# Retention: the product of masked scores and values in high and low parts, one modulation step and one reciprocal moved

## The reference, cut to what matters

```
s   = einsum(q, k) * decay            # masked scores, per head
o   = einsum(s, v)                    # the product that is changed
var = mean(square(o - mean(o)))       # group norm over the 512 channels
ro  = (o - mu) * rsqrt(var + eps);  ro = ro * gn_g + gn_b
ret_out = (silu(rg) * ro) @ w_ret_out
mod = silu(c) @ w_ada + b_ada         # "modulation", a matrix-vector product
```

## Time and profile before

| | us |
|---|---|
| runs before, median of 3 | 2944.29 |
| profiled execution | 2945.46 |
| its span | 2943.7 |
| PE busy | 2844.9 (97%) |
| DVE busy | 1749.9 (59%) |
| ACT busy | 989.7 (34%) |

### The profile page before, as it was taken

The page is one execution under the profiler, slowest core; times in us unless marked ns, Lnnn a source line. Parts: engine busy times, 40 slices in busy tenths (PEclk is TensorE's granted clock), DMA queues, the critical chain, the costliest instruction groups (busy, mean ns, idle before and its releaser), DMA issues.

```text
span 2943.7 us, 37223 instructions
## 1 busy us (share of the span) xinstructions
PE 2844.9 (97%) x15519; PEld 2444.4 (83%) x15519; DVE 1749.9 (59%) x2406; ACT 989.7 (34%) x1371; POOL 121.2 (4%) x157
## 2 busy tenths in 40 slices
PE   6999999999899999999989999999999988999999
PEld 5888887979788888789878888888888977888887
DVE  6655755554566777566487565665555348454454
ACT  4333333232333222332276232222213337332222
POOL 0100000000001100000000000000000000000000
PEclk9999999999999999999989999999999999999999
DMA  7343444545234644343510212233322251223232
GB/s 247 125 135 106 130 146 143 174 117 159 88 116 119 198 149 130 100 130 114 135 38 15 86 53 92 92 100 96 100 65 83 68 115 37 65 79 93 93 108 72
DMA packets 267507, 317.17 MB, mean 108 GB/s; under 512 B 24859, under 2 KB 236203, under 8 KB 267340
## 3 DMA queue, kind: packets, MB, share of 16 engines
q1 hardware_dynamic: 240764, 230.60, 25.6%
q0 software_dynamic: 19456, 72.00, 8.3%
q10 hardware_dynamic: 7120, 12.20, 1.3%
HBM read 291.96 MB, written 11.27 MB: 103 GB/s over the span
## 4 chain that ended last, share of the span: by engine, by line
PE 89%; DVE 5%; ACT 2%; DVEq 2%; issue 1%; DMA 0%; ACTq 0%
PE psum L621 26%; PE psum L623 26%; PE psum L622 26%; PE psum L1037 2%; PE psum L851 1%; PE psum L1049 1%; DVE dneg L2436 1%; DVE sba L2447 1%; DVE n_t L1887 1%; PE psum L921 1%; PE psum L838 1%; ACT pt L1704 1%; PE psum L1128 1%; DVE w_lo L1899 1%; PE psum L1118 0%
## 5 line engine op out<-in xcount | busy, mean ns | idle before, releaser
L621 PE MATMUL psum<-hs_hi,w_hi 128*128 128x512 f32 x1632 | 646.7, 396 | 7.6 <-DVE hs_lo L1891 5.3
L1899 DVE TENSOR_TENSOR w_lo<-raw,w_hi 128x2048 fp32r<-128x2048 f32 (+1 forms) x246 | 435.5, 1770 | 367.3 <-ACT w_hi L1270 255.6
L622 PE MATMUL psum<-hs_hi,w_lo 128*128 128x512 f32 x1632 | 638.0, 391 | 0.0
L623 PE MATMUL psum<-hs_lo,w_hi 128*128 128x512 f32 x1632 | 637.6, 391 | 0.0
L621 PEld LDWEIGHTS psum<-hs_hi,w_hi 128*128 128x128 f32 x1632 | 307.8, 189 | 80.5 <-issue 7.8
L623 PEld LDWEIGHTS psum<-hs_lo,w_hi 128*128 128x128 f32 x1632 | 307.8, 189 | 65.3
L622 PEld LDWEIGHTS psum<-hs_hi,w_lo 128*128 128x128 f32 x1632 | 308.1, 189 | 62.0 <-issue 1.0
L1959 DVE SCALAR_TENSOR_TENSOR ada_acc<-ada_raw,csil,ada_acc 128x512 f32<-128x512 f32 x392 | 279.6, 749 | 37.2 <-DMA ada_raw<-in_w_ada 19.3
L1280 ACT CAST w_hi<-raw 128x2048 fp32r<-128x2048 f32 (+1 forms) x138 | 191.3, 1386 | 325.9 <-PE psum L623 314.6
L621 PE MATMUL psum<-mid_hi,w_hi 128*128 128x512 f32 x768 | 300.7, 392 | 0.0
L622 PE MATMUL psum<-mid_hi,w_lo 128*128 128x512 f32 x768 | 299.1, 389 | 0.0
(11 more groups left out here) (361 smaller groups left out, 4548.6 us busy)
## 6 DMA issues: line engine op xcount, KB each, us to landing
raw<-in_w_in SPq DMA_DIRECT2D x56, 1024.0 KB, 5.2
ada_raw<-in_ada_w POOLq DMA_DIRECT2D x96, 512.0 KB, 4.0
raw<-in_w_ff SPq DMA_DIRECT2D x48, 1024.0 KB, 5.5
raw<-in_w_ff SPq DMA_DIRECT2D x96, 512.0 KB, 3.4
ada_raw<-in_w_ada POOLq DMA_DIRECT2D x32, 512.0 KB, 4.3
raw<-in_w_in SPq DMA_DIRECT2D x24, 512.0 KB, 4.6
raw<-in_w_ret_out SPq DMA_DIRECT2D x16, 512.0 KB, 3.5
raw<-in_w_out SPq DMA_DIRECT2D x8, 1024.0 KB, 5.0
```

What stands on the lines that cost most here:

```text
L621: pe.matmul(dst, lhi, rhi, start=start, stop=False)
L622: pe.matmul(dst, llo, rhi, start=False, stop=False)
L623: return pe.matmul(dst, lhi, rlo, start=False, stop=stop)
L1899: low = dve.tensor_tensor(w_lo[par][:, k0:kt], raw[par][:, k0:kt], w_hi[par][:, k0:kt].bitcast(F32), ALU.subtract)
```

## The change

Three edits in each head. First, line 851 becomes three fp32r products of high and low parts. ACT rounds centred values and masked scores (`v_hi`, `s_hi`), DVE takes the remainders (`v_lo`, `s_lo`, in place), PE waits for both remainders (`pv_split`). Second, each slot of the modulation moves one place back: two slots stood ahead of the gate unit's remainder and now one; seven stood ahead of the sum of squares and now six. Third, the reciprocal stands ahead of the last slot instead of behind it. Some semaphores are merged (`rope_in` with `decay_in`, `x_in` with `ctx_in`); the waits then count higher.

```
 # PE
-pe.wait_ge(s_masked, 4 * h + 4)
-pe.wait_ge(v_centred, h + 1)
+pe.wait_ge(pv_split, 2 * h + 2)
...
-mm = pe.matmul(dst[:, jb * P:S], rv[:, jb, e * P:(e + 1) * P], qk_raw[:, jb, 0:S - jb * P], ...)
+pe.matmul(dst[:, jb * P:S], v_hi[:, jb, v_], s_hi[:, jb, 0:w], ...)
+pe.matmul(dst[:, jb * P:S], v_hi[:, jb, v_], s_lo[:, jb, 0:w], ...)
+mm = pe.matmul(dst[:, jb * P:S], v_lo[:, jb, v_], s_hi[:, jb, 0:w], ...)
 # ACT, behind the last weight copy before the gate
+act.wait_ge(v_centred, h + 1)
+act.copy(v_hi[:], rv[:]).then_inc(pv_hi, 1)
+act.wait_ge(s_masked, 4 * h + 4)
+act.copy(s_hi[:], qk_raw[:]).then_inc(pv_hi, 1)
 # DVE, behind the masks
-for s in range(2):
-    ada_slot(s, h, False)
+for j, (low, whole, high) in enumerate(((v_lo, rv, v_hi), (s_lo, qk_raw, s_hi))):
+    dve.wait_ge(pv_hi, 2 * h + j + 1)
+    dve.tensor_tensor(low[:], whole[:], high[:].bitcast(F32), ALU.subtract).then_inc(pv_split, 1)
+ada_slot(0, h, False)
 lo(n + 5, 1)
-for s in range(2, 7):
+for s in range(1, 6):
     ada_slot(s, h, False)
 dve.wait_ge(o_evac, 4 * h + 4)
 ...                                    # sum of squares
 lo(n + 6, 0)
-ada_slot(7, h, False)
+ada_slot(6, h, False)
 dve.wait_ge(gstd_done, h + 1)
 dve.reciprocal(gn_rstd[:], gn_std[:]).then_inc(gn_factor, 1)
+ada_slot(7, h, False)
```

More of the change, by code:

```diff
@@ L227, in build @@
         z_lo = at("z_lo", [P, 4, S], F32R, F1 + 8192)
+        v_hi = at("v_hi", [P, 4, RET_DV], F32R, F1)
+        s_hi = at("s_hi", [P, 4, S], F32R, F1 + 8192)
         accr = at("accr", [P, KT, S], F32, F1 + 16384)
@@ L231, in build @@
         rv = at("rv", [P, 4, RET_DV], F32, F1 + 49152)
+        s_lo = at("s_lo", [P, 4, S], F32R, F1 + 32768)
+        v_lo = at("v_lo", [P, 4, RET_DV], F32R, F1 + 49152)
         ro = at("ro", [P, 4, S], F32, F1 + 57344)
@@ L369, in build @@
         vrow_in, vrow3_in = sem("vrow1_in"), sem("vrow3_in")
-        x_in = sem("x_in")
+        tokens_in = sem("tokens_in")
         rel_in = sem("rel_in")
@@ L390, in build @@
         csq_ready, csq_used, x_scaled = sem("ctx_squares_ready"), sem("ctx_squares_used"), sem("x_scaled")
-        rope_in, decay_in = sem("rope_in"), sem("decay_in")
+        tables_in = sem("retention_tables_in")
+        pv_hi, pv_split = sem("ret_pv_hi"), sem("ret_pv_split")
         roped, s_done, s_masked, pv_done, o_evac, v_centred, gsq_done, var_done, gstd_done, zf_done, zhi_done, zlo_done = (
@@ L407, in build @@
         rpb_in, nb_out = [sem("rpb_in0"), sem("rpb_in1")], [sem("nb_out0"), sem("nb_out1")]
-        ctx_in, ct_done, ct_read = sem("ctx_in"), sem("ct_done"), sem("ct_read")
+        ct_done, ct_read = sem("ct_done"), sem("ct_read")
         cc_in, rope2_in, ws_in, dft_in, ln_in, bb_in = (
@@ L484, in _ @@
             ada_block(1)
-            sp.dma_start(x_tok[:], d["x"].rearrange("b (t p) n -> p (b t) n", p=P)).then_inc(x_in, 16)
+            sp.dma_start(x_tok[:], d["x"].rearrange("b (t p) n -> p (b t) n", p=P)).then_inc(tokens_in, 16)
             ada_block(3)
@@ L514, in _ @@
             sp.wait_ge(hs_ready, 8)
-            sp.dma_start(rope[:], d["rope1"]).then_inc(rope_in, 16)
-            sp.dma_start(decay[:], d["decay"][0]).then_inc(decay_in, 16)
+            sp.dma_start(rope[:], d["rope1"]).then_inc(tables_in, 16)
+            sp.dma_start(decay[:], d["decay"][0]).then_inc(tables_in, 16)
             ret_head(0, 0, False, True)
@@ L519, in _ @@
                 sp.wait_ge(s_masked, 4 * h)
-                sp.dma_start(decay[:], d["decay"][bass.ds(h, 1)].rearrange("a p s -> (a p) s")).then_inc(decay_in, 16)
+                sp.dma_start(decay[:], d["decay"][bass.ds(h, 1)].rearrange("a p s -> (a p) s")).then_inc(tables_in, 16)
                 ret_head(h, FU["heads"] + 10 * (h - 1), True)
@@ L550, in load_context @@
                 sp.wait_ge(gemm_done, R(FU["ff"]))
-                sp.dma_start(c_tok[:], d["ctx_2"].rearrange("b (t p) n -> p (b t) n", p=P)).then_inc(ctx_in, 16)
+                sp.dma_start(c_tok[:], d["ctx_2"].rearrange("b (t p) n -> p (b t) n", p=P)).then_inc(tokens_in, 16)
             feed(sp, load, wf1, wf2, FU["ff"], load_context)
@@ L775, in _ @@
             ada0_sums(1, range(0, 4))
-            pe.wait_ge(x_in, 16)
+            pe.wait_ge(tokens_in, 16)
             x_tiles(range(2))
@@ L850, in ret_head @@
                     for jb in range(4):
-                        mm = pe.matmul(dst[:, jb * P:S], rv[:, jb, e * P:(e + 1) * P], qk_raw[:, jb, 0:S - jb * P],
-                                       start=jb == 0, stop=jb == 3, skip_group_check=True)
+                        v_, w = slice(e * P, (e + 1) * P), S - jb * P
+                        pe.matmul(dst[:, jb * P:S], v_hi[:, jb, v_], s_hi[:, jb, 0:w], start=jb == 0, stop=False, skip_group_check=True)
+                        pe.matmul(dst[:, jb * P:S], v_hi[:, jb, v_], s_lo[:, jb, 0:w], start=False, stop=False, skip_group_check=True)
+                        mm = pe.matmul(dst[:, jb * P:S], v_lo[:, jb, v_], s_hi[:, jb, 0:w], start=False, stop=jb == 3,
+                                       skip_group_check=True)
                     mm.then_inc(pv_done, 1)
@@ L1007, in context_tiles @@
             def context_tiles():
-                pe.wait_ge(ctx_in, 16)
+                pe.wait_ge(tokens_in, 32)
                 for k in range(KT):
@@ L1375, in _ @@
             hi(0)
-            act.wait_ge(x_in, 16)
+            act.wait_ge(tokens_in, 16)
             token_root(x_tok, 4, n_junk)
@@ L2075, in ret_head @@
                 if not with_out:
-                    dve.wait_ge(rope_in, 16)
+                    dve.wait_ge(tables_in, 32)
                 rotate(n, 0)
@@ L2092, in ret_head @@
                 if with_out:
-                    dve.wait_ge(decay_in, 16 * h + 16)
+                    dve.wait_ge(tables_in, 32 + 16 * h)
                 else:
-                    dve.wait_ge(decay_in, 16)
+                    dve.wait_ge(tables_in, 32)
                 for jb, (src, c0) in enumerate(((X0, 0), (X1, 0), (C0, 0), (C0, 256))):
```

## The result

| | before | after |
|---|---|---|
| median of 6 runs each, taken together | 2942.31 | 2955.07 |
| lowest to highest | 2937.28 to 2946.96 | 2952.42 to 2962.25 |
| profiled execution, span | 2945.46, 2943.7 | 2956.27, 2954.5 |
| start of the table of biases behind the fourth head (line 878, now 885) | 447.31 | 458.07 |

After is slower: ratio 1.0052, 95% interval 1.0038 to 1.0066, which is 11 to 19 us. The forecast was 2949.1 us, its range 2941.5 to 2953.5; the result lies above the range, with the sign of the likeliest case and more than twice its size.

The account below looks back on a forecast made before the run. PE, busy 97%, was taken to bound the kernel, with DVE's chain deciding after the change. Head losses of 2.0 + 0.4 + 0.4 + 2.0 = 4.8 us on 2944.3 gave 2949.1 us, range 2941.5 to 2953.5.

Parts of the forecast that it names:

- the likeliest case: Load of slot 3 takes 5.3 to 6.6 us, so the kernel is slower, 2947 to 2951 us; chance 0.65.
- PE's product: Line 851's product in each head: 7.6 us instead of 8.5, 0.95 us saved.
- the further 0.1: First fp32r unit behind the product: its first step of 0.32 us becomes 0.23, sparing PE 0.1 more a head.
- B: Rival: 128-wide matmuls take 0.06 us and DVE's chain is not late; 6.6 us gained, 2937.7 us; chance 0.06.
- C: Rival: 128-wide fp32r as slow as fp32 (0.21 us), PE spared nothing; 2949.2 us, inside the forecast's chance.
- The input in time: Second head's product: `s_lo` done at 204.9, PE wants it at 208.56; 3.7 us of slack hide the split.
- The DVE chain and D: Second head: D, the transfer time of slot 3's load, is 6.0 us, so the q unit's `w_lo` comes at 229.5.
- rival D: Load of slot 5 also takes 6.0 us instead of 4.0; 12.8 us slower, 2957 us; chance 0.12, halfway cases included.
- The step that failed: Second head's q unit: late `w_lo` cancels PE's saving of 1.05 us and loses 0.4 us more.
- First head: Loses 2.0 us, because `z_lo` comes late; the 0.8 us from its late `w_lo` is included.
- The `lam` chain: Behind the first head: memset starts 4.1 us later, so `z_lo` comes at 150.6 where PE wants it at 148.52.
- Fourth head: Loses 2.0 us: next unit's `w_lo` moves from 438.61 to 440.6, `z_f32` follows it and line 878 waits.

Follow-up runs that it names:

- work in the wait: Kernel after, plus twelve matmuls on constants (1.34 us) on PE behind the small product, ahead of each q unit; 2951.44 us, ratio 1.0039 to before.
- order alone: Kernel before with its fp32 product, but the slots and the reciprocal in the changed order; 2947.13 us, ratio 1.0025 to before.
- split alone: Kernel after's product in three parts, with slots and reciprocal where they stood before; 2957.01 us, ratio 1.0060 to before.
- one-product kernel: Kernel after with only the high-by-high product, the two products with a remainder left out on PE; 2954.12 us, ratio 1.0049 to before.
- slot 5 behind the remainder: Kernel after with modulation slot 5 moved from ahead of the sum of squares to behind the q unit's `w_lo`; 2951.30 us, ratio 1.0035 to before.
- SP's load held back to the third tile: Kernel after, SP's load of the next k unit's weight waiting for the product's third output tile; 2950.54 us, ratio 1.0037 to before.

## Why the prediction was off, step by step

- **PE's product**: right. 7.62 us a head for 7.6; 0.06 and 0.11 us from start to start at 128 wide (213.86, 213.92, 214.03), 0.17 at 384. Of the further 0.1 only 0.04 goes, since the first matmul behind the product still takes 0.28 (219.91 to 220.19) where it took 0.32; so PE is spared 0.97 us a head and not 1.05. Rivals B and C fall with it.
- **The input in time**: right. `s_lo` is done at 208.6, PE asks at 212.29, and there is no wait on the split.
- **The DVE chain and D**: right. D is 6.4 where I took 6.0, slot 5's load keeps 4.0 (rival D's mechanism did not happen; its 2957 lies near the result for another reason), `w_lo` comes at 229.8 for 229.5. That SP's load lengthens slot 3's was a guess from two rows; holding it back showed it, 6.4 to 4.0.
- **The step that failed**: "With D = 6.0 the `w_lo` comes at 229.5: PE's saving of 1.05 is gone and 0.4 us more is lost." The lateness was priced as time that PE stands, with the q unit behind it at its 0.23 pace. It isn't: 1.15 us of standing is followed by some 3.4 us at half clock, 1.64 us more in each q unit. The clock, which the sum put at nothing without a word, is the term that failed. The kernel with work in the wait takes exactly this away, with `w_lo` as late as ever. In heads two and three it is 3.3 of the 4.1 us that the sum missed there; the remaining 0.4 a head is the size by which D was short (6.4 for 6.0). The trace of before held the warning. Behind line 878, PE's view by stretches reads:

```profile
450.00:455.00 5.00, 5.00 (x17) 3.95 (x17) 0.09 (x1) 4.29 (x3) 0.47 (x1) 0.66 0.75 241
```

The clock is 0.66 in 5 us in which PE is fully busy, behind 3 us of small products and a wait of 0.25. I had read the earlier trace rows only up to that wait. But the wait by itself would not have told it: the one wait of 1.2 us in the earlier trace rows stands between matmuls 512 wide, and behind it they stay 0.23 apart, with the granted clock at 1.00 from 50 to 70 us:

```profile
55.95 0.50 PE L621 MATMUL psum<-hs_hi,w_hi 128*128 128x512 f32 x1 [1.18 <-DVE w_lo L1899]
...
56.53 0.40 PE L623 MATMUL psum<-hs_lo,w_hi 128*128 128x512 f32 x1
56.76 0.40 PE L621 MATMUL psum<-hs_hi,w_hi 128*128 128x512 f32 x1
```

- **First head**: 1.4 us more than forecast. The `lam` chain was right (`z_lo` done at 150.86, forecast 150.6), but PE came to it only at 151.20 because of its own q unit, so the `z_lo` wait I expected wasn't there; and the z units then lost 1.1 us to `w_lo` of the second and third z unit, which stand behind the late `z_lo` on DVE; the order alone shows 1.35 us there. In after:

```profile
163.00 0.50 PE L626 MATMUL psum<-z_hi,w_hi 128*128 128x512 f32 x1 [0.57 <-DVE w_lo L1910]
```

- **Fourth head**: 2.1 for 2.0, the number right and its cause only half. The `z_f32` chain is late by that much (the order alone shows it, 1.66 us of wait), but in after PE is as late by itself, and line 885 waits 0.3 us as before. Two delays side by side, of which either would do.
- **The edits**: I asked what the edits cost together. The experiments part them: split alone +14.4 in the stage (1.3 of it the one long q unit), order alone +4.5, both +10.8. The order edit costs by itself and repairs under the split; its sign depends on the other edit, which the prediction didn't ask.
- **The rest**: the split's gain, 3.7 us in PE, was there, covered by a chain that PE no longer sets (the one-product kernel).

The miss against the median, 2955.1 to 2949.1, is 6.0 us: 5.6 from the stage (10.4 less 4.8), and the remaining 0.4 lies within the spread of the runs. That the two fit so well is partly luck, since the forecast stood on a median of 2944.3 and the six runs of before have 2942.3.

## What to carry to other kernels

Price a new wait of PE that stands behind small products twice: the time it stands, and the half clock of the work behind it (here 1.15 + 1.64 us, once 2.9). Look in the trace for what follows the same products already, and not only for a wait of the same length, since between wide matmuls such waits cost here nothing more than themselves; or give PE cheap work in the gap. When an edit puts work on a helper engine with slack, follow the loads that it releases later and see which large transfer of another queue they now fall behind: here one load's neighbour decided 8.5 us of the stage. And test the edits of a change apart, since one may be good only in the company of the other.

## What the runs showed of the hardware

- The clock's fall isn't settled by the length of a wait. Between wide matmuls the pace stayed at 0.23 behind waits of 1.2 us (near 56 us in every kernel), 1.59 (ahead of the last output tile of the one-product kernel, in each head) and 2.69 (slot 5 behind the remainder):

```profile
139.76 0.36 PE L803 MATMUL psum<-ada_acc,fold 128*128 128x16 f32 x2 [2.69 <-DVE mod L2003]
```

- Behind the eight matmuls one column wide, all eight waits of 1.15 us (after and the split alone) were followed by the lower level, and so were those of 0.89 and 0.91 with SP's load held back to the third tile; the one of 0.94 in the third head of that run wasn't. Behind the products of the table of biases it fell with hardly a wait (0.25 us, before) and with none (after, at 486.07: clock 0.70 from 490 to 495). The 3.5 us of standing in the one-product kernel lowered it ahead of any small product (0.84 from 228 to 231.5, then 0.50). All the other falls seen here stand right behind small products. That these are the reason was not tested: no run changes them and keeps the wait.
- The price is not fixed. Behind 1.15 us of standing a q unit took 7.0 to 7.2 us, once 8.45. In the one-product kernel, where PE stood 3.5 us ahead of the small product and 0.34 behind it, the unit took 7.1 to 7.5, but the small product too ran at half clock (0.50 from 231.5 on), so the lower level lasted longer, some 6 us.
- A load of 128 x 1024 values by POOL takes 4.0 us, from issue until DVE starts on it, with no large load under way, 6.4 to 6.7 when issued about 2 us behind SP's 1 MB load, 5.7 at 3.3 us behind and 4.9 at 5.3 us behind; issued 2.2 us ahead of SP's it took 4.1. The Trainium skill ("DMA: Bandwidth & Descriptors", section "Issuing engines are not separate DMA queues") says that transfers started by different engines run on the same 16 DMA engines and interleave. These lengths agree with it.
- The first fp32r matmul 128 wide of a group takes 0.06 us from start to start and the next two 0.11 each: the next instruction's weights are the same in the first step (`v_hi` twice) and new in the others. That the repeat is the reason was not tested.
